# Banded attention: another order of scores, value products and turns on TensorE, and moved work at the begin and end of its stage

## The chip, the cores and the metric

The kernel runs on one core of one Trainium2 chip. The metric is device time in microseconds. Times before: 1762.6 us, the median of three runs (1760.01 to 1762.82).

## The reference

One layer of a hybrid block on 1024 latent tokens of width 1024, with 256 context tokens: a projection to all branches, differential attention, pooling, windowed attention, a merge, and a feed-forward block. The change touches the third branch, windowed attention with sink logits, and what is computed beside it:

```python
rel = jnp.arange(band)[None, :] - WA_BLOCK - jnp.arange(WA_BLOCK)[:, None]
band_ok = jnp.abs(rel) <= WA_WINDOW
def one(args):
    i, qblk = args
    kb = lax.dynamic_slice_in_dim(kp, i * WA_BLOCK, band, axis=1)
    vb = lax.dynamic_slice_in_dim(vp, i * WA_BLOCK, band, axis=1)
    ...
    s_band = jnp.einsum('bqkgd,bjkd->bkgqj', qblk, kb).astype(jnp.float32) * scale
    s_band = jnp.where(ok, s_band, -jnp.inf)
    s_ctx = jnp.einsum('bqkgd,bjkd->bkgqj', qblk, kc).astype(jnp.float32) * scale
    p = sink_softmax(jnp.concatenate([s_band, s_ctx], axis=-1), sink_g)
    vv = jnp.concatenate([vb, vc], axis=1)
    return jnp.einsum('bkgqj,bjkd->bqkgd', p.astype(v.dtype), vv)
```

There are 8 query heads in 2 key heads, a head is 64 wide, a block is 128 queries, and a query sees the blocks at its left and right, its own, and the context.

## The kernel before

The stage is `window`. It cuts the work into 32 units: key head (16 units each), block of 128 queries, pair of heads. A unit has two heads, s = 0 and 1, and four or five tiles of 128 keys: two of context, and two (first and last block) or three of the band. The units run in a software pipeline of 35 steps. On TensorE, step i before the change issues the scores of unit i for both heads (lines 1634 to 1645, five matmuls a head, the last adds the mask), the value products of unit i-2 (line 1673, 2 x 4 or 2 x 5 pairs of matmuls of 64 columns in the array), and the turns of unit i-1 (line 1659): transposes of the two heads' exponentials and of one tile of reciprocals, in three parts of at most four tiles.

The other engines follow their own programs of the same steps. ScalarE does the exponential of head 0, the exponential of head 1 (line 1752), the exponential of the sinks (1757), the copy of part 0 of the turns of unit i-1 out of PSUM (1763), and the high part of the output of unit i-2 (1769). VectorE does the maximum of head 0 (1914), in the first nine units the low part of an output (1859), the reciprocals of unit i-1 (1926) and their widening (1852), the maximum of head 1, in the first nine the sinks (1846), the output of unit i-2 (1942), and the copies of parts 1 and 2 (1931). From unit 9 on POOL does the low part, the widening and the sinks.

Order between engines is by semaphores alone. The four upper PSUM banks form a ring (`ring`, `slot`, `use`): the value product, the three turn parts, and in some steps a fifth user take the next bank each, and each waits until the bank's last user has been copied out. Fifth users are the conditioning sums in steps 0 and 1, the row sums in steps 4, 5, 5 and 6 (line 1696), a pool product in steps 7, 10, ... 28 (helper lines 78 to 80) and a branch turn in steps 9, 12, ... 30 (line 1681). A product waits besides for the copies of all three of its turn parts.

At the stage's begin POOL adds and multiplies two rows (lines 1869 and 1870, twice) and splits the pool weights into a high and a low part (1873, 1875), for which the sync queue (SP) loads them (1592). ScalarE takes a square root (1832) whose reciprocal VectorE forms (1984). At its end the first merge product (`merge_first`, helper lines 106 to 109) is issued in two pieces in steps 32 and 33.

Of the kernel before, what the change touches and what calls it, by code (L numbers as in the profile page):

```python
# [1449 lines left out]
def window(nc, sem, block, banks, io, keep):  # L1450
# [6 lines left out]
    UN = WA_KV * KU  # L1457
# [6 lines left out]
    with ExitStack() as ctx:  # L1464
# [103 lines left out]
        @block.sync  # L1568
        def _(sp):
            def load_v(kv, landed):  # L1570
                v = io["vals"][DA_HEADS].rearrange("t p (g d) -> g p t d", g=WA_KV)[kv]
                sp.dma_start(val[kv][:, 2:TT, :], v[:, 0:TL, :]).then_inc(landed, 16)
                sp.dma_start(val[kv][:, 0:2, :], v[:, TL:TT, :]).then_inc(landed, 16)

            sp.wait_ge(*att["cleared"])
            sp.sem_inc(passed, 1)
            load_v(0, v_in)
            for done in ("products", "last_out", "squares"):
                sp.wait_ge(*att[done])
            for i in range(2):  # L1580
                sp.dma_start(row_in_sb[2 * i], io["b_ada"][0:1, (2 + 3 * i) * D:(3 + 3 * i) * D].to_broadcast([P, D])).then_inc(rows_in, 16)
                sp.dma_start(row_in_sb[2 * i + 1], io["norm_g"][1 + 2 * i:2 + 2 * i, :].to_broadcast([P, D])).then_inc(rows_in, 16)
            sp.wait_ge(*att["late"])
            for n in range(2):
                for part, a in ((0, 0), (1, HD)):
                    src = io["qk"][10 + n, part].rearrange("(s d) n -> d s n", d=HD)
                    for s, y in enumerate((y_hi, y_lo)):
                        sp.dma_start(y[2][a:a + HD, 2 + n, :].bitcast(F32), src[:, s, 0:SEQ]).then_inc(q1_in, 16)
            sp.wait_ge(sums_read, 4)
            load_v(1, v1_in)  # L1590
            load_window_keys(io, sp, 1, (kc1[:, 0, :], kc1[:, 1, :]), CTX, SEQ, kc1_in)
            sp.dma_start(pw[:], io["pool_w"]).then_inc(pw_in, 16)
            sp.wait_ge(late_ready, 1)
            sp.dma_start(io["late_row"], late_row[0:1]).then_inc(late_out, 16)
            for n in range(2):
                for s in range(2):
                    sp.wait_ge(sc_done[s], (10, 16)[n])
                cols = slice(CTX + n * HALF, CTX + (n + 1) * HALF)
                load_window_keys(io, sp, 1, (k_st[:, cols], k_sw[:, cols]), HALF, n * HALF, k1_in[n])
            for j in range(2):  # L1600
                sp.dma_start(keep["b_raw"][j][:], io["w_br"][j]).then_inc(keep["b_in"][j], 16)
            sp.wait_ge(late_out, 16)

        @block.tensor
        def _(pe):
# [2 lines left out]
                pe.wait_ge(free[b], used + 1)  # L1608
                return b, banks[4 + b]

            def scores(u):
                kv, blk, pair = at(u)
                if u == 0:
                    pe.wait_ge(qk_in, 16 * (8 + WA_GROUP))
                    pe.wait_ge(const_ready, 2)
                if u == KU:
                    pe.wait_ge(q1_in, 16 * 8)
                    pe.wait_ge(kc1_in, 16 * 4)
                    pe.wait_ge(k1_in[0], 16 * 4)
                if u == KU + 6:  # L1620
                    pe.wait_ge(k1_in[1], 16 * 4)
                band = tiles_of(u)[2]
                width = (len(tiles_of(u)) - 2) * P
                for s in range(2):
                    if u == 0:
                        for done in att["exps"][s]:
                            pe.wait_ge(*done)
                    else:
                        pe.wait_ge(exp_done[s], u + 1)
                    here = slice(blk * P, (blk + 1) * P)  # L1630
                    q = (y_hi, y_lo)[s][2][:, 2 + pair, here] if kv else q_st[pair][:, s, here]
                    keys = (kc1[:, 0, :], kc1[:, 1, :]) if kv else (k_st[:, 0:CTX], k_sw[:, 0:CTX])

                    pe.matmul(banks[2 * s][:, CTX:HALF], q, keys[0], start=True, stop=False)
                    pe.matmul(banks[2 * s][:, CTX:HALF], q, keys[1], start=False, stop=True)
                    out, cols = banks[2 * s + 1][:, 0:width], slice(band * P, band * P + width)
                    pe.matmul(out, q, k_st[:, cols], start=True, stop=False)
                    pe.matmul(out, q, k_sw[:, cols], start=False, stop=False)
                    sides = slice(0, 3, 2)
                    if width == BAND:  # L1640
                        mm = pe.matmul(out.rearrange("p (a n) -> p a n", n=P)[:, sides, :], ident_r[:],
                                       mask_r[:].rearrange("p (a n) -> p a n", n=P)[:, sides, :], start=False, stop=True)
                    else:
                        m0 = (band - 2 - (blk - 1)) * P
                        mm = pe.matmul(out, ident_r[:], mask_r[:, m0:m0 + width], start=False, stop=True)
                    mm.then_inc(sc_done[s], 1)
# [68 lines left out]
            cond_sums(1)  # L1715
            for i in range(1, STEPS):
                if 2 <= i < UN:
                    scores(i)
                if i == UN + 1:
                    first["product"](pe, 0, range(2, BC))  # L1720
                if 0 <= i - 2 < UN:
                    products(i - 2)
                if i == UN:
                    for s in range(2):
                        pe.wait_ge(exp_done[s], UN + 1)
                    pe.wait_ge(da_lo_ready, GROUPS)
                    first["product"](pe, 0, range(2))
                if 0 <= i - 1 < UN:
                    turn(i - 1)
                if i in POOL_STEPS:  # L1730
# [131 lines left out]
        def _(pool):  # L1862
# [1 line left out]
            pool.memset(ones, 1.0).then_inc(ones_ready, 1)  # L1864
            pool.wait_ge(rows_in, 64)
            ch = Chain(pool, pool_step)
            for i, out in enumerate((gate_row[:], late_row)):
                pool.wait_ge(sums_read, 2 * i + 2)
                ch.link(pool.tensor_tensor(out, out, row_in_sb[2 * i], ALU.add))
                ch.link(pool.tensor_tensor(out, out, row_in_sb[2 * i + 1], ALU.mult))  # L1870
            pool.sem_inc(late_ready, 1)
            pool.wait_ge(pw_in, 16)
            pool.tensor_copy(pw_hi[:], pw[:]).then_inc(pw_ready, 1)
            pool.wait_ge(pw_ready, 1)
            pool.tensor_tensor(pw_lo[:], pw[:], pw_hi[:].bitcast(F32), ALU.subtract).then_inc(pw_ready, 1)
            pool.wait_ge(rms_ready, 1)

            def normed(g):
# [30 lines left out]
        def _(v):  # L1909
# [39 lines left out]
            for i in range(STEPS):  # L1949
# [20 lines left out]
                if i < UN:  # L1970
                    maximum(ch, i, 1)
                    if i < POOL_FROM:
                        sinks(v, i)
                if i == 3:
                    v.wait_ge(*att["squares"])
                    v.tensor_scalar(ss[:], ss[:], 1.0 / DA_V, EPS, ALU.mult, ALU.add).then_inc(ss_ready, 1)
# [2 lines left out]
                if 0 <= i - 1 < UN:  # L1979
                    copy_out(i - 1, 1)  # L1980
                    copy_out(i - 1, 2)
                if i == 3:
                    v.wait_ge(root_ready, 1)
                    v.reciprocal(ss[:], ss[:]).then_inc(rms_ready, 1)


def merge_first(nc, sem, banks, keep):
# [1381 lines left out]
```

## Time and profile before

| | |
|---|---|
| median of the runs | 1762.6 us |
| profiled execution | 1762.77 us, span 1760.8 us |
| mean granted clock of TensorE | 0.994 |
| TensorE busy | 1715.9 us, 97% |
| VectorE busy | 1212.0 us, 69% |
| ScalarE busy | 808.4 us, 46% |
| POOL busy | 809.2 us, 46% |

The first four rows are of the whole kernel; the stage that is changed covers some 170 us of it, near 715 to 887 us from the span's start. TensorE is busy nearly always, in the sense that some matmul is in flight; a gap on it is time in which it waited. The granted clock is a share of full speed. In rows in order of time a matmul's length is its way through the array, longer than the distance to the next matmul's start, so costs are taken from start to start.

### The profile page before, as it was taken

What the parts mean: (1) busy time and instruction counts of PE and PEld (TensorE: products, weight loads), DVE (VectorE), ACT (ScalarE), POOL (GpSimd) and SP (SyncE); (2) the same over time, 40 slices, a digit from 0 to 9 for tenths busy, and PEclk for the clock granted to TensorE, in tenths of its full rate; (3) what the DMA queues carried; (4) which work ended last, traced back from release to release, by engine and by line L of the source; (5) the groups of instructions that cost most, each with busy time, mean ns of one, the idle gap of its engine ahead of it and who ended that gap; (6) DMA issues with size and microseconds to landing.
All of it is one profiled execution on the core that took longest, in us unless ns stands there. A gap on an engine that the chain in (4) does not pass through costs nothing. (4 is left out here: it accounts for less than half of the span.)

```text
span 1760.8 us, 25882 instructions
## 1 busy us (share of the span) xinstructions
PE 1715.9 (97%) x9180; PEld 1448.3 (82%) x9180; DVE 1212.0 (69%) x1651; ACT 808.4 (46%) x1593; POOL 809.2 (46%) x579
## 2 busy tenths in 40 slices
PE   8999999999998999989999999899999999999998
PEld 6997888888887999878888878678888888878886
DVE  3628688879958999778733466875665665575767
ACT  3435333435637888657711155633333333354453
POOL 1407577776533899435522232465555555400000
PEclk9999999999999999989999999999999999999999
DMA  9233233435767655512053332132233233386734
GB/s 352 86 109 137 98 120 154 154 147 182 273 170 212 171 139 139 159 32 73 2 196 120 120 133 89 73 131 96 95 116 134 95 107 119 119 280 214 250 100 179
DMA packets 98568, 249.87 MB, mean 142 GB/s; under 512 B 12321, under 2 KB 26017, under 8 KB 98338
## 3 DMA queue, kind: packets, MB, share of 16 engines
q1 hardware_dynamic: 98466, 248.52, 42.3%
q8 instruction: 63, 1.03, 0.2%
q14 instruction: 39, 0.32, 0.1%
HBM read 183.07 MB, written 65.41 MB: 141 GB/s over the span
## 5 line engine op out<-in xcount | busy, mean ns | idle before, releaser
L750 POOL TENSOR_TENSOR ring<-raw_w,ring 128x512 fp32r<-128x512 f32 x120 | 186.9, 1575 | 137.5 <-ACT ring L621 137.5
L78 PE MATMUL psum<-h_hi,ring 128*128 128x512 f32 x400 | 155.9, 390 | 2.7 <-ACT z L667 2.0
L80 PE MATMUL psum<-h_hi,ring 128*128 128x512 f32 x400 | 155.6, 389 | 0.0
L79 PE MATMUL psum<-h_lo,ring 128*128 128x512 f32 x400 | 155.6, 389 | 0.0
L78 PE MATMUL psum<-u_slot 128*128 128x512 f32 x308 | 120.4, 391 | 1.3 <-DVE u_slot L2976 1.2
L80 PE MATMUL psum<-u_slot 128*128 128x512 f32 x308 | 120.2, 390 | 0.0
L79 PE MATMUL psum<-u_slot 128*128 128x512 f32 x308 | 119.9, 389 | 0.0
L621 ACT ACTIVATE ring<-raw_w 128x512 fp32r<-128x512 f32 x120 | 72.5, 625 | 100.2 <-DVE raw_w L915 31.8
L1406 DVE TENSOR_REDUCE mx<-psum 128x1 f32<-128x1280 f32 x64 | 95.1, 1487 | 7.6 <-PE psum L1292 6.9
L1339 ACT ACTIVATE e<-psum,neg_m 128x1280 f32<-128x1280 f32 x64 | 85.0, 1328 | 31.2 <-DVE neg_m L1407 31.2
L2575 POOL TENSOR_TENSOR cut_lo<-i_raw,cut_hi 128x512 fp32r<-128x512 f32 x44 | 66.8, 1519 | 59.3 <-ACT cut_hi L2430 59.3
L78 PEld LDWEIGHTS psum<-h_hi,ring 128*128 128x128 f32 x400 | 75.1, 188 | 19.2 <-issue 3.9
L2575 POOL TENSOR_TENSOR cut_lo<-stage,cut_hi 128x512 fp32r<-128x512 f32 x40 | 59.8, 1495 | 64.0 <-ACT cut_hi L2430 64.0
L80 PEld LDWEIGHTS psum<-h_hi,ring 128*128 128x128 f32 x400 | 75.1, 188 | 15.7
L79 PEld LDWEIGHTS psum<-h_lo,ring 128*128 128x128 f32 x400 | 75.1, 188 | 15.6
L1291 PE MATMUL psum<-k_st,q_st 128*128 128x512 f32 (+1 forms) x192 | 74.3, 387 | 5.8 <-ACT e L1339 4.8
L1305 PE MATMUL psum<-val,at 128*128 128x128 f32 x640 | 76.7, 275 | 0.0
L78 PE MATMUL psum<-b_hi,cut_hi 128*128 128x512 f32 x176 | 69.5, 395 | 4.8 <-POOL cut_lo L2575 2.3
L1305 PEld LDWEIGHTS psum<-val,at 128*128 128x128 f32 x640 | 74.0, 192 | 0.0
L78 PE MATMUL psum<-m_parts,i_hi 128*128 128x512 f32 x176 | 69.6, 395 | 0.3 <-PE psum L80 0.3
L78 PE MATMUL psum<-i_t_hi,cut_hi 128*128 128x512 f32 x176 | 68.5, 389 | 1.3 <-POOL i_lo L2575 1.3
L78 PEld LDWEIGHTS psum<-u_slot 128*128 128x128 f32 x308 | 57.8, 188 | 14.5 <-DVE u_slot L2981 1.6
(419 smaller groups left out, 5198.7 us busy)
## 6 DMA issues: line engine op xcount, KB each, us to landing
raw_w<-in_w_pairs SPq DMA_DIRECT2D x40, 512.0 KB, 4.7
qk_dram<-room SPq DMA_DIRECT2D x26, 512.0 KB, 3.6
room<-in_w_ada SPq DMA_DIRECT2D x24, 512.0 KB, 5.7
gates_dram<-ost SPq DMA_DIRECT2D x24, 512.0 KB, 3.0
b_g<-gates_dram SPq DMA_DIRECT2D x8, 1536.0 KB, 7.5
stage<-in_w_ff SPq DMA_DIRECT2D x22, 512.0 KB, 5.9
i_raw<-in_w_ff SPq DMA_DIRECT2D x22, 512.0 KB, 5.0
f_dram<-h SPq DMA_DIRECT2D x22, 512.0 KB, 3.4
```

What stands on the lines that cost most here:

```text
L78: pe.matmul(out, sh, mh, start=first, stop=False, skip_group_check=onto)
L79: pe.matmul(out, sh, ml, start=False, stop=False, skip_group_check=onto)
L80: return pe.matmul(out, sl, mh, start=False, stop=last, skip_group_check=onto)
L621: act.activation(w_hi[i], source(p, i), ACT.Copy).then_inc(w_hi_ready, 1)
L750: pool.tensor_tensor(w_lo[i], source(p, i), w_hi[i].bitcast(F32), ALU.subtract).then_inc(w_lo_ready, 1)
L1291: pe.matmul(out, q, k_st[j][:, s, c0:c0 + w], start=True, stop=False)
L1305: mm = pe.matmul(bank[:, 2 * P:3 * P], at[t % 2][:, k, :], val[t // TL % 2][:, k, :], start=(k == 0), stop=(k == TT - 1))
L1339: act.activation(e[i % 2][s][:], psum[:, 3 * s * HALF:3 * s * HALF + TOK], ACT.Exp, scale=SCALE, bias=neg_m[:, i % 2, s:s + 1], accum_out= ...
L1406: ch.link(v.tensor_reduce(mx[:, s:s + 1], psum[:, 3 * s * HALF:3 * s * HALF + TOK], AX.X, ALU.max))
L2575: pool.tensor_tensor(f_lo[i], source(q, i), f_hi[i].bitcast(F32), ALU.subtract).then_inc(fw_lo_ready, 1)
```

## The change

On TensorE the scores of the two heads are taken apart: a step now issues the scores of head 0, the value products, the scores of head 1, and the turns. The names in the rows are the program's: `y_hi` and `y_lo` hold the queries of the second key head, `k_st` and `wa_kc` keys, `we` the exponentials, `wpt` the turned ones. TensorE, a step of a unit with five tiles, before:

```order
L1635 MATMUL psum<-wa_kc,y_hi 128x256
L1637 MATMUL psum<-k_st,y_hi 128x384
L1638 MATMUL psum<-k_st,y_hi 128x384
L1641 MATMUL psum<-wa_mask_r,wa_ident_r 128x2x128
L1634 MATMUL psum<-wa_kc,y_lo 128x256
L1635 MATMUL psum<-wa_kc,y_lo 128x256
L1637 MATMUL psum<-k_st,y_lo 128x384
L1638 MATMUL psum<-k_st,y_lo 128x384
L1641 MATMUL psum<-wa_mask_r,wa_ident_r 128x2x128
L1673 MATMUL psum<-wpt,wa_val 64x128 x10
L1659 MATMUL psum<-ident,we 128x128 x10
L1659 MATMUL psum<-ident,wpt 128x128
```

TensorE, the same place, now:

```order
L1635 MATMUL psum<-wa_kc,y_hi 128x256
L1637 MATMUL psum<-k_st,y_hi 128x384
L1638 MATMUL psum<-k_st,y_hi 128x384
L1641 MATMUL psum<-wa_mask_r,wa_ident_r 128x2x128
L1673 MATMUL psum<-wpt,wa_val 64x128 x10
L1634 MATMUL psum<-wa_kc,y_lo 128x256
L1635 MATMUL psum<-wa_kc,y_lo 128x256
L1637 MATMUL psum<-k_st,y_lo 128x384
L1638 MATMUL psum<-k_st,y_lo 128x384
L1641 MATMUL psum<-wa_mask_r,wa_ident_r 128x2x128
L1659 MATMUL psum<-ident,we 128x128 x10
L1659 MATMUL psum<-ident,wpt 128x128
```

The ten rows of the products stood behind both heads' scores, and stand between them now; the turns stay last.

At the stage's end, in step 32 (`b_hi_first` and `b_lo_first` are merge weights), TensorE before:

```order
L1659 MATMUL psum<-ident,wpt 128x128
L1673 MATMUL psum<-wpt,wa_val 64x128 x8
L106 MATMUL psum<-y_hi,b_hi_first 128x512
L107 MATMUL psum<-y_lo,b_hi_first 128x512
L106 MATMUL psum<-y_hi,b_hi_first 128x512
L107 MATMUL psum<-y_lo,b_hi_first 128x512
L109 MATMUL psum<-y_hi,b_lo_first 128x512 x2
```

and now:

```order
L1645 MATMUL psum<-wa_mask_r,wa_ident_r 128x256
L1659 MATMUL psum<-ident,we 128x128 x8
L1659 MATMUL psum<-ident,wpt 128x128
L106 MATMUL psum<-y_hi,b_hi_first 128x512
L107 MATMUL psum<-y_lo,b_hi_first 128x512
L106 MATMUL psum<-y_hi,b_hi_first 128x512
L107 MATMUL psum<-y_lo,b_hi_first 128x512
```

The product of unit 30 stood ahead of the first piece of the merge product, and stands behind it now.

POOL at the stage's begin (`gate_row` and `early` are the two rows, `wa_pw` the pool weights), before:

```order
L1869 TENSOR_TENSOR gate_row<-gate_row,rows 128x1024
L1870 TENSOR_TENSOR gate_row<-gate_row,rows 128x1024
L1869 TENSOR_TENSOR early<-early,rows 128x1024
L1870 TENSOR_TENSOR early<-early,rows 128x1024
L1873 CAST pool_w_hi<-wa_pw 128x512
L1875 TENSOR_TENSOR pool_w_lo<-wa_pw,pool_w_hi 128x512
L1881 TENSOR_TENSOR on<-o,o_squares 128x512
```

and now:

```order
L1872 TENSOR_TENSOR gate_row<-gate_row,rows 128x1024
L1873 TENSOR_TENSOR gate_row<-gate_row,rows 128x1024
L1877 CAST pool_w_hi<-wa_pw 128x512
L1879 TENSOR_TENSOR pool_w_lo<-wa_pw,pool_w_hi 128x512
L1872 TENSOR_TENSOR early<-early,rows 128x1024
L1873 TENSOR_TENSOR early<-early,rows 128x1024
L1887 TENSOR_TENSOR on<-o,o_squares 128x512
```

The split of the pool weights has moved ahead of the second row. On the sync queue the load of the pool weights has moved ahead of six loads for the second key head, and on VectorE the reciprocal of the squares from the end of step 3 to step 5, ahead of its output. The programs of ScalarE and of the other steps are as they were.

```diff
--- before.py
+++ after.py
@@ -1587,9 +1587,9 @@
                     for s, y in enumerate((y_hi, y_lo)):
                         sp.dma_start(y[2][a:a + HD, 2 + n, :].bitcast(F32), src[:, s, 0:SEQ]).then_inc(q1_in, 16)
             sp.wait_ge(sums_read, 4)
+            sp.dma_start(pw[:], io["pool_w"]).then_inc(pw_in, 16)
             load_v(1, v1_in)
             load_window_keys(io, sp, 1, (kc1[:, 0, :], kc1[:, 1, :]), CTX, SEQ, kc1_in)
-            sp.dma_start(pw[:], io["pool_w"]).then_inc(pw_in, 16)
             sp.wait_ge(late_ready, 1)
             sp.dma_start(io["late_row"], late_row[0:1]).then_inc(late_out, 16)
             for n in range(2):
@@ -1608,7 +1608,7 @@
                 pe.wait_ge(free[b], used + 1)
                 return b, banks[4 + b]
 
-            def scores(u):
+            def scores(u, heads=range(2)):
                 kv, blk, pair = at(u)
                 if u == 0:
                     pe.wait_ge(qk_in, 16 * (8 + WA_GROUP))
@@ -1621,7 +1621,7 @@
                     pe.wait_ge(k1_in[1], 16 * 4)
                 band = tiles_of(u)[2]
                 width = (len(tiles_of(u)) - 2) * P
-                for s in range(2):
+                for s in heads:
                     if u == 0:
                         for done in att["exps"][s]:
                             pe.wait_ge(*done)
@@ -1715,16 +1715,18 @@
             cond_sums(1)
             for i in range(1, STEPS):
                 if 2 <= i < UN:
-                    scores(i)
+                    scores(i, [0])
                 if i == UN + 1:
                     first["product"](pe, 0, range(2, BC))
-                if 0 <= i - 2 < UN:
-                    products(i - 2)
                 if i == UN:
                     for s in range(2):
                         pe.wait_ge(exp_done[s], UN + 1)
                     pe.wait_ge(da_lo_ready, GROUPS)
                     first["product"](pe, 0, range(2))
+                if 0 <= i - 2 < UN:
+                    products(i - 2)
+                if 2 <= i < UN:
+                    scores(i, [1])
                 if 0 <= i - 1 < UN:
                     turn(i - 1)
                 if i in POOL_STEPS:
@@ -1864,15 +1866,19 @@
             pool.memset(ones, 1.0).then_inc(ones_ready, 1)
             pool.wait_ge(rows_in, 64)
             ch = Chain(pool, pool_step)
-            for i, out in enumerate((gate_row[:], late_row)):
+
+            def row(i, out):
                 pool.wait_ge(sums_read, 2 * i + 2)
                 ch.link(pool.tensor_tensor(out, out, row_in_sb[2 * i], ALU.add))
                 ch.link(pool.tensor_tensor(out, out, row_in_sb[2 * i + 1], ALU.mult))
-            pool.sem_inc(late_ready, 1)
+
+            row(0, gate_row[:])
             pool.wait_ge(pw_in, 16)
             pool.tensor_copy(pw_hi[:], pw[:]).then_inc(pw_ready, 1)
             pool.wait_ge(pw_ready, 1)
             pool.tensor_tensor(pw_lo[:], pw[:], pw_hi[:].bitcast(F32), ALU.subtract).then_inc(pw_ready, 1)
+            row(1, late_row)
+            pool.sem_inc(late_ready, 1)
             pool.wait_ge(rms_ready, 1)
 
             def normed(g):
@@ -1971,6 +1977,9 @@
                     maximum(ch, i, 1)
                     if i < POOL_FROM:
                         sinks(v, i)
+                if i == 5:
+                    v.wait_ge(root_ready, 1)
+                    v.reciprocal(ss[:], ss[:]).then_inc(rms_ready, 1)
                 if i == 3:
                     v.wait_ge(*att["squares"])
                     v.tensor_scalar(ss[:], ss[:], 1.0 / DA_V, EPS, ALU.mult, ALU.add).then_inc(ss_ready, 1)
@@ -1979,9 +1988,6 @@
                 if 0 <= i - 1 < UN:
                     copy_out(i - 1, 1)
                     copy_out(i - 1, 2)
-                if i == 3:
-                    v.wait_ge(root_ready, 1)
-                    v.reciprocal(ss[:], ss[:]).then_inc(rms_ready, 1)
 
 
 def merge_first(nc, sem, banks, keep):
```

## Rows read from the trace of the kernel before

**Rows 1.** Stretches: length, busy us (instructions) by engine, granted clock, DMA share, GB/s

```profile
730.32:778.76 48.44, 39.04 (x291) 31.71 (x290) 33.59 (x89) 24.34 (x58) 12.38 (x8) 0.86 0.41 105
778.76:872.78 94.02, 93.79 (x935) 84.86 (x933) 77.20 (x203) 71.84 (x184) 45.20 (x85) 1.00 0.13 41
872.78:886.40 13.62, 12.54 (x107) 10.35 (x106) 6.18 (x16) 5.77 (x15) 6.40 (x10) 1.00 0.01 1
745.00:749.00 4.00, 3.78 (x16) 3.00 (x18) 2.53 (x8) 2.22 (x7) 0.00 (x0) 0.66 0.48 100
```

**Rows 2.** Waits of the window stage: who for whom; us, times, longest

```profile
PE psum L78 <- POOL pool_w_lo L1875: 3.5, 1, 3.5
PE psum L1659 <- DVE wpt L1852: 3.1, 3, 1.2
PE psum L1696 <- DVE wpt L1942: 2.4, 2, 1.2
DVE o_squares L1984 <- ACT o_squares L1832: 1.7, 1, 1.7
```

**Rows 3.** Order of time, TensorE, step 20: start, us, what [idle before <-releaser]

```profile
824.49 0.48 PE L78 MATMUL psum<-y_hi,pool_w_hi 128*128 128x512 f32 x1
...
825.26 0.28 PE L1634 MATMUL psum<-wa_kc,y_hi 128*128 128x256 f32 x1
...
825.84 0.28 PE L1641 MATMUL psum<-wa_mask_r,wa_ident_r 128*128 128x256 f32 x1
...
826.75 1.31 PE L1673 MATMUL psum<-wpt,wa_val 128*64 128x128 f32 x20
828.00 1.31 PE L1659 MATMUL psum<-ident,we 128*128 128x128 f32 x10
...
829.17 0.37 PE L1634 MATMUL psum<-wa_kc,y_hi 128*128 128x256 f32 x1
```

**Rows 4.** The same step on VectorE and ScalarE

```profile
826.16 0.82 DVE L1914 TENSOR_REDUCE wmx<-psum 128x1 f32<-128x640 f32 x1 [0.56 <-PE psum L1641]
...
828.38 0.28 DVE L1942 TENSOR_TENSOR wpt<-psum,wpt 128x128 f32<-128x128 f32 x1
...
827.27 0.80 ACT L1752 ACTIVATE we<-psum,wneg_m 128x640 f32<-128x640 f32 x1 [0.41 <-DVE wneg_m L1916]
...
828.50 0.80 ACT L1752 ACTIVATE we<-psum,wneg_m 128x640 f32<-128x640 f32 x1 [0.35 <-DVE wneg_m L1916]
...
829.38 0.59 ACT L1763 ACTIVATE wpt<-psum 128x512 f32<-128x512 f32 x1
```

**Rows 5.** The same view near the stage's end: POOL, VectorE, TensorE

```profile
875.99 1.27 POOL L1887 TENSOR_TENSOR y_lo<-on,y_hi 128x512 fp32r<-128x512 f32 x1
...
876.50 0.89 DVE L1931 COPY wpt<-psum 128x512 f32<-128x512 f32 x2 [0.61 <-PE psum L1659]
...
877.64 1.09 PE L1673 MATMUL psum<-wpt,wa_val 128*64 128x128 f32 x16 [1.07 <-DVE wpt L1931]
```

**Rows 6.** ScalarE, the exponential of a unit with four key tiles

```profile
811.89 0.69 ACT L1752 ACTIVATE we<-psum,wneg_m 128x512 f32<-128x512 f32 x1
```

**Rows 7.** The opening: TensorE, VectorE, sync queue, POOL

```profile
751.68 1.88 PE L1696 MATMUL psum<-late_rows,early 128*128 128x512 f32 x4
...
756.33 2.08 DVE L1852 COPY wpt<-wrec 128x128 f32<-128x128 f32 x1
...
762.68 0.38 SPq L1572 DMA_DIRECT2D wa_val<-vals_dram  x1
...
766.57 0.59 SPq L1592 DMA_DIRECT2D wa_pw<-in_pool_w  x1
...
769.52 0.61 POOL L1873 CAST pool_w_hi<-wa_pw 128x512 fp32r<-128x512 f32 x1 [1.90 <-DMA wa_pw<-in_pool_w]
770.21 1.26 POOL L1875 TENSOR_TENSOR pool_w_lo<-wa_pw,pool_w_hi 128x512 fp32r<-128x512 f32 x1
```

**Rows 8.** TensorE's 20 products at the lower clock

```profile
748.71 1.78 PE L1673 MATMUL psum<-wpt,wval 128*64 128x128 f32 x20
```

## The prediction

> **What bounds the kernel now.** I read the table of stages first. The window stage splits into an opening (steps 2 to 8, 48.44 us), a steady part (steps 9 to 30, 94.02 us) and an end (13.62 us) [rows 1]. A step i issues the scores of unit i, the value products of unit i-2 and the turns (transposes) of unit i-1, so a steady step lasts 94.02/22 = 4.27 us. In the steady part TensorE is busy 93.79 of 94.02 us at clock 1.00: there it is the bound. In the opening it is busy 39.04 of 48.44 us, at a mean granted clock of 0.86, so it waits for others and then also runs at the lower of its two levels (1.2 and 2.4 GHz).
>
> Next come the waits [rows 2]: 3.5 us at the first pool product for the split of the pool weights, 3.1 us at the last turn of a unit for the widened reciprocals, 2.4 us at row sums for the output that frees their bank. VectorE lost 1.7 us waiting for the square root. That is the opening. After step 9 almost nothing stands there.
>
> Last I read one steady step on TensorE [rows 3] and on VectorE and ScalarE [rows 4] in order of time, because the new order changes who waits there. The reader is to see in [rows 4] the exponential of head 1 at 828.50, and right behind it on ScalarE, in program order, the copy of turn part 0 at 829.38. The products of the same unit need that copy. Today it ends at 829.97, while TensorE is busy with the scores of both heads of the next step from 829.17, 10 matmuls lasting from 825.26 to 826.75 in the step shown, 1.49 us, plus 0.08 after turns. So the products are due at about 830.75: the copy is hidden with about 0.8 us to spare.
>
> **Part one: the order in the steady steps.** Nothing is added or removed, no matmul is longer. But the scores of head 1 now stand behind the products, so (a) the products have only one head's scores, 0.66 to 0.78 us, in front of them instead of two, and (b) the exponential of head 1 comes later than before relative to the turns. ScalarE's order is not changed: it still does exponential head 0, exponential head 1, sinks, and only then the copy of part 0. That closes a loop: scores of head 1 (step i), maximum, exponential, copy of part 0 (unit i-1), products (unit i-1, step i+1), scores of head 1 (step i+1). Its links for a unit with five key tiles:
> - last matmul of a head's scores to the reduce: 825.84 to 826.16, 0.32 [rows 3, 4]
> - reduce to its exponential: 826.16 to 827.27, 1.11 [rows 4]
> - exponential of head 1 to the copy of part 0: 828.50 to 829.38, 0.88 [rows 4]
> - that copy: 0.59 [rows 4]
> - end of a copy to the products it releases: the row 876.50 + 0.89 = 877.39 to 877.64, 0.25 [rows 5]
> - the 20 products: 826.75 to 828.00, 1.25 [rows 3]
> - scores of one head up to their last matmul: 825.26 to 825.84, 0.58 [rows 3]
>
> The sum is 4.98 us. The other way round TensorE has, between the last matmul of the scores of head 1 and the next products, only 0.11 + turns 1.17 + 0.78 = 2.1 us of work, and the copy is there after 3.15: about 1 us of idle per step. VectorE's own copies of parts 1 and 2 don't set it: its output starts 0.12 ahead of the exponential of head 1 (828.38 against 828.50), so at 0.32 + 1.11 - 0.12 = 1.31, ends at 1.59, and both copies, 1.16 for five tiles (0.89 for four, [rows 5]), end at 2.75. With four key tiles the exponential takes 0.69 for 0.80 [rows 4, 6], 0.11 less; the reduce (512 keys for 640) is about 0.13 shorter, the products (16 for 20) 0.22, the scores 0.11: the loop is 4.41.
>
> A pool product (0.77: 824.49 to 825.26 [rows 3]) uses the bank that the output on VectorE frees, at 1.59 + 0.15 = 1.74 after that last matmul. Then 1.74 + 0.77 + 0.78 + 0.1 = 3.4 against the copy's 3.15: 0.25 more in each of 7 steps, 1.75. A branch turn, four transposes, is shorter and fits.
>
> Of the 22 steps I count 17 at five tiles and 5 at four: 17 x 4.98 + 5 x 4.41 + 1.75 = 108.5, against 94.0. **Term A is +14.5 us.** Its bounds: 0 if the loop is somehow hidden, 14.5 plus about 22 if the clock stays low (second rival). I take the loop, since every link has a row in this very stage.
>
> **Part two: the new places at the begin.** Seven steps of the loop, with the first not held back (about 0.9 less), are 34.0 us. What comes on top, step by step:
> - Steps 4 and 5, +2.7. Two row sums took 1.32 us, from 751.68 to the scores at 753.00 [rows 7], so three are 2.0, behind the bank's release at about 1.74; the rest is my allowance for ScalarE's function tables, which it loads around the square root. The reciprocal that VectorE waited 1.7 us for now stands in step 5, where its input is long there; what is late next is the row sum's bank.
> - Step 6, +2.9: the widening copy on VectorE took 2.08 us, until the add on POOL had ended (756.33 + 2.08 = 758.41) [rows 7], and the maximum of head 1 and all that hangs on it stood behind. That add stays where it is. With the fourth row sum and some half clock I take 2.9.
> - Step 7, +2.2: pool weights. The issue moves ahead of six DMAs of the sync queue. It was issued at 766.57 and used at 769.52, 2.95 later; the first of the six went out at 762.68, and there it stands now, 3.9 us sooner [rows 7], and on POOL the split (769.52 to 770.21, and 1.26) stands ahead of the two adds of the second row. TensorE waits about 2.2 instead of 3.5. The six loads behind it are wanted from step 16 on: no cost.
> - Step 8, +0.25. The second row's adds now overlap this step and the reciprocals' users; the late row goes out some 5 us later, and is wanted in step 9 by ScalarE's branch copy, which is about as late as that: nothing, or up to 1 us.
>
> Sum 34.0 + 8.05 = 42.05 against 48.44: **term B is -6.4 us**, bounds -12 (neither row sums nor half clock cost anything) to -1 (the clock is as low as before).
>
> **Part three: the end.** Before, the products of unit 30 waited 1.07 us for VectorE's copy [rows 5]. Now the first half of the merge product (2.87 us) stands before them; but it needs the low part of the last branch, on POOL behind the sinks of the last unit. These end about 0.32 + 1.11 + 0.2 = 1.6 us after the last score; the subtract takes 1.27 [rows 5]. So it starts about 2.9 us after the scores, of which the turns cover 1.1: the wait of 1.07 becomes one of about 1.8. From the start of the last scores I get 0.1 + 0.5 + 0.2 + 1.25 + 0.5 + 2.9 + 2.87 + 1.03 + 0.96 + 2.87 + 1.1 = 14.3 to 14.7 against 13.62. **Term C is +1.0**, bounds -1.1 to +2.
>
> **Sum.** +14.5 - 6.4 + 1.0 = +9.1 us. What follows is bound by TensorE without a gap, so the shift is carried to the end. The profiled execution took 1762.77 us (span 1760.8), 0.2 over the median 1762.6; I forecast 1772, own range 1766 to 1778.
>
> **Rivals.**
> 1. Faster than before: the loop never decides. ScalarE has 0.41 and 0.35 us of idle ahead of its exponentials [rows 4], and DVE's second reduce used to queue behind the first; if spreading them let the copy of part 0 start before TensorE comes to the products (no later than 1.3 us after the last score; the links say 2.3), term A is 0 to +1 and the time is 1757. Against: the links are a chain, none can start earlier. Chance 0.08.
> 2. The clock falls in the steady part. After 745 TensorE ran four us at 0.66 [rows 1], behind turns and two waits of up to 1.2 us of [rows 2]. At the lower level 20 products took 1.78 for 1.31 [rows 8] and a head's scores about twice 0.58. The loop would be about 1.0 longer: 22 us if always, 11 if half the time, 1783 to 1794. For: now every step has turns and then a wait. Against: scores stand between turns and wait here, the gap is a single one of about 1 us, and the like gap at 877 left the clock at 1.00. Chance 0.14.
> 3. The loop is only half as dear (some 0.45 us a step, because a released product starts sooner than 0.25 or the reduce sooner than 0.32): A is +7, the time 1764. Chance 0.13.
>
> Rival 2 is what the Trainium skill would have (TensorE: Matmul & The Clock Gate, "A second HAM failure mode: psum-queue depth-cycling"): a TensorE that idles briefly between groups of matmuls in every iteration is seen to swing between both clock levels. By that rule it would be about 1788; the trace has full clock through the small gaps of the steady part and half clock only after the pairs of long ones, so I keep it a rival.
>
> **How the numbers follow.** Forecast 0.65, rivals 0.08, 0.14 and 0.13. The range 1763 to 1786 leaves out rival 1, the slow half of rival 2 and little of rival 3. A measurement of this kernel tells about 0.2%, 3.5 us: slower has the forecast, rival 2 and a part of rival 3, 0.82; the same 0.10; faster 0.08.
>
> **What would show it.** In the steady part of the new profile TensorE idles about 1 us per step before line 1673, released by ScalarE's copy (line 1765 now), and a step lasts about 5.0 us. The wait at the first pool product is near 2 us, VectorE's wait for the square root is gone, the opening is 42 us. I am wrong if TensorE has no such wait, or if the granted clock in the steady part is under 0.95.

## The result and the profile of the changed kernel

The changed kernel takes 1776.48 us (median of 4 runs, 1774.01 to 1779.46), the kernel before in the same series 1762.53. The ratio is 1.0079, with a 95% interval of 1.0065 to 1.0093: slower by 0.8%. Forecast were 1772.0, with a range of 1763 to 1786. The profiled execution took 1775.1 us (span 1773.1, mean granted clock 0.995), 12.3 more than that of before.

First the stretches, cut at the same points as [rows 1]: opening, steady part and end (length, then busy us of TensorE, its weight loads, VectorE, ScalarE, POOL, granted clock, DMA share, GB/s).

```profile
732.40:775.24 42.84, 34.84 (x292) 28.70 (x290) 32.34 (x85) 22.83 (x54) 12.35 (x7) 0.96 0.45 119
775.24:884.70 109.46, 98.78 (x934) 86.29 (x932) 80.26 (x208) 72.37 (x186) 44.75 (x85) 1.00 0.10 35
884.70:899.33 14.63, 12.78 (x108) 10.35 (x106) 5.46 (x16) 6.19 (x17) 6.71 (x10) 1.00 0.00 1
```

The opening went from 48.44 to 42.84 us (-5.6), the steady part from 94.02 to 109.46 (+15.4), the end from 13.62 to 14.63 (+1.0). Together +10.8. In the steady part the same matmuls are issued, the clock is 1.00 as before, and TensorE now leaves 10.7 us unused where it left 0.2. The other 5.0 us are busy time (98.78 for 93.79) of the same instructions. About 2.2 of them are the first score of head 1, which now follows another group and takes 0.22 to the next matmul instead of 0.12, 22 times. For the rest I have only an estimate: the last matmul ahead of a gap counts for its whole way through the array, 0.28 in the rows below, and not for the 0.12 to the next one's start, which over some 21 gaps makes about 3.

The waits of TensorE name the owners (total us, times, longest). This is the steady part alone:

```profile
PE psum L1673 <- ACT wpt L1765: 5.5, 7, 1.0
PE psum L1681 <- DVE wpt L1948: 2.4, 7, 0.8
PE psum L1673 <- DVE wpt L1937: 1.4, 1, 1.4
PE psum L78 <- DVE wpt L1948: 1.2, 7, 0.2
```

In the kernel before TensorE idled 0.2 us in all of this stretch. Over the opening and the end the list has these too:

```profile
PE psum L78 <- POOL pool_w_lo L1879: 2.2, 1, 2.2
PE psum L106 <- POOL y_lo L1893: 1.9, 1, 1.9
PE psum L1659 <- DVE wpt L1854: 1.0, 1, 1.0
```

The wait for the pool weights was 3.5 and is 2.2, the last turns' wait for the reciprocals was 3.1 and is 1.0, and VectorE's wait for the square root (1.7 in [rows 2]) is gone.

How the steady part fills 15 us with only seven waits at the products is to be seen in order of time. These are the rows of TensorE and of its partners for one step without a branch turn or a pool product (start, us, what [idle before <-releaser]):

```profile
832.79 0.28 PE L1641 MATMUL psum<-wa_mask_r,wa_ident_r 128*128 128x256 f32 x1
...
834.21 0.80 ACT L1754 ACTIVATE we<-psum,wneg_m 128x640 f32<-128x640 f32 x1 [1.26 <-DVE wneg_m L1922]
...
835.09 0.58 ACT L1765 ACTIVATE wpt<-psum 128x512 f32<-128x512 f32 x1
...
835.73 1.31 PE L1673 MATMUL psum<-wpt,wa_val 128*64 128x128 f32 x20 [0.76 <-ACT wpt L1765]
...
837.66 0.28 PE L1641 MATMUL psum<-wa_mask_r,wa_ident_r 128*128 128x256 f32 x1
...
837.98 0.82 DVE L1920 TENSOR_REDUCE wmx<-psum 128x1 f32<-128x640 f32 x1 [1.02 <-PE psum L1641]
...
839.09 0.80 ACT L1754 ACTIVATE we<-psum,wneg_m 128x640 f32<-128x640 f32 x1 [1.75 <-DVE wneg_m L1922]
...
839.97 0.59 ACT L1765 ACTIVATE wpt<-psum 128x512 f32<-128x512 f32 x1
```

This is the chain of the prediction, link for link. From the last matmul of head 1's scores to the reduce 0.32 (837.66 to 837.98), to the exponential 1.11, to the copy of part 0 0.88 (839.09 to 839.97, and 834.21 to 835.09). The copy ends at 835.67 and the products start at 835.73, then 1.24 for them and 0.69 for a head's scores. Against [rows 3, 4] the next rows of TensorE show what it costs; they are the products of four successive steps:

```profile
840.70 1.31 PE L1673 MATMUL psum<-wpt,wa_val 128*64 128x128 f32 x20
...
850.75 1.31 PE L1673 MATMUL psum<-wpt,wa_val 128*64 128x128 f32 x20 [0.76 <-ACT wpt L1765]
```

Those between start at 835.73 (above) and 845.88. So a step without extra work takes 4.88 us (830.85 to 835.73), the one with a branch turn 4.97 (835.73 to 840.70), the one with a pool product 5.18 (840.70 to 845.88), and the next plain one 4.87 again. In the kernel before the same three were 4.00 (826.75 to 830.75), 4.44 (to 835.19) and 4.69 (to 839.88). Before, a step was as long as its work; now all steps are about as long as the loop. Only one in three shows a long wait at the products. In the other two TensorE has already waited at the turn or at the pool product, for VectorE's output of the same chain:

```profile
839.40 0.63 PE L1681 MATMUL psum<-ident,on 128*128 128x128 f32 x4 [0.25 <-DVE wpt L1948]
...
844.28 0.50 PE L78 MATMUL psum<-y_hi,pool_w_hi 128*128 128x512 f32 x1 [0.16 <-DVE wpt L1948]
```

Last the end. The products of unit 30 do not wait any more; the first half of the merge product waits instead, for POOL's subtract behind the last unit's sinks:

```profile
888.90 1.27 POOL L1893 TENSOR_TENSOR y_lo<-on,y_hi 128x512 fp32r<-128x512 f32 x1
...
890.45 0.47 PE L106 MATMUL psum<-y_hi,b_hi_first 128*128 128x512 f32 x1 [1.85 <-POOL y_lo L1893]
```

### The profile page after: what moved, and what is told of

It reads as the page before. It is cut to its first block and busy times, and to the rows that moved or that the text cites. A ratio compares the mean times of both kernels' runs of the same rounds, so it can differ in the third digit from the quotient of the medians.

```text
span 1773.1 us, 25885 instructions
## 1 busy us (share of the span) xinstructions
PE 1718.1 (97%) x9180; PEld 1448.8 (82%) x9180; DVE 1212.0 (68%) x1651; ACT 807.8 (46%) x1593; POOL 809.1 (46%) x579
## 5 line engine op out<-in xcount | busy, mean ns | idle before, releaser
L1920 DVE TENSOR_REDUCE wmx<-psum 128x1 f32<-128x640 f32 (+1 forms) x64 | 50.5, 789 | 42.2 <-PE psum L1641 28.9
L1754 ACT ACTIVATE we<-psum,wneg_m 128x640 f32<-128x640 f32 (+1 forms) x64 | 49.1, 768 | 58.0 <-DVE wneg_m L1922 56.4
```

The costliest lines, as they stand in the source:

```text
L1754: act.activation(e[u % 2][s][:, 0:keys], psum[:, 2 * s * HALF + CTX:2 * s * HALF + CTX + keys], ACT.Exp, scale=SCALE, bias=neg_m[:, u % 2, ...
L1920: ch.link(v.tensor_reduce(mx[:, s:s + 1], psum[:, 2 * s * HALF + CTX:2 * s * HALF + CTX + keys], AX.X, ALU.max))
```

## The experiments

Times are medians; each ratio is against the kernel before on the same chip, with its 95% interval. Lengths of the stage are from the first matmul of the scores of unit 2, unit 9 and unit 31 and the first matmul of the merge product behind the last products, as above. They come from one profiled execution each.

**1. The order alone.** The kernel before with TensorE's new order and nothing else.

```
-  scores(i)
+  scores(i, [0])
   ...
   products(i - 2)
   ...
+  scores(i, [1])
   turn(i - 1)
```

> Only the new order on TensorE (scores of head 0, products, scores of head 1, turns), with the old places at the stage's begin and end. Theory (the loop over ScalarE's copy of part 0 sets the step): steady part (steps 9 to 30) about 109 us against 94.0, opening about 48 as before (its waits are others'), end +0.8; in all +15.5 us, about 1778. Rival (the order costs little, and most of the 14 us comes from the moved places or from work ahead of the stage): under +5 us.

Measured: 1780.05 us (1779.26 to 1782.52), ratio 1.0096 (1.008 to 1.0111). Opening 47.69, steady part 108.88, end 14.08. In its steady part the waits of TensorE are:

```profile
PE psum L1673 <- ACT wpt L1765: 5.4, 7, 0.9
PE psum L1681 <- DVE wpt L1944: 2.4, 7, 0.8
PE psum L1673 <- DVE wpt L1933: 1.0, 1, 1.0
```

The list has the pool products too, with 1.2 in 7 waits as in the changed kernel. The order alone makes the whole loss, +14.9 of steady part, with the same owners. The opening stays near that of before (48.44), so it is the new places that shorten it.

**2. The places alone.** The changed kernel with the scores of both heads together again.

```
-  scores(i, [0])
+  scores(i)
   ...
-  scores(i, [1])
```

> Only the new places at the begin and the end, with both heads' scores ahead of the products in every step as before. Theory: steady part 94 to 95 us, opening about 40 against 48.4 (pool weights, reciprocal of the squares, and with these less half clock), end as before; in all -7 us, about 1755, and both parts add up to the change (+15.5 - 7 against a measured +14 would leave some 5 us to explain). Rival (the places bring nothing, since the next wait is as late): within 2 us of before.

Measured: 1758.75 us (1755.52 to 1761.67), ratio 0.9973 (0.9963 to 0.9983): faster than before. Opening 40.86, steady part 95.30, end 13.63. The loop is gone from the waits. The gain is 5.0 us where about 7 had been expected. The opening is 0.9 longer than expected, and the steady part is 1.3 longer than before, since its first step takes 5.82 instead of 4.53. Just ahead of that step TensorE waits for VectorE's widening of reciprocals, and within it for ScalarE:

```profile
774.88 0.33 PE L1659 MATMUL psum<-ident,wpt 128*128 128x128 f32 x1 [1.19 <-DVE wpt L1852]
776.78 0.39 PE L1634 MATMUL psum<-k_st,k_sw 128*128 128x256 f32 x1 [0.86 <-ACT we L1752]
```

Why VectorE is late there, experiment 6 shows.

**3. ScalarE's copy first.** The changed kernel, but ScalarE copies part 0 of the turned weights between its two exponentials. If the place behind the second exponential makes the loop, the wait must move.

```
   exp(i, 0)
+  if 2 <= i and i - 1 < UN: copy_out(i - 1, 0)
   exp(i, 1)
   ...
   sinks(i)
-  copy_out(i - 1, 0)
+  if i == 1: copy_out(0, 0)
```

> The changed kernel, with ScalarE's copy of turn part 0 ahead of its exponential of head 1. Theory: the copy is out of the loop, but VectorE's copies of parts 1 and 2 end only 0.15 us a step earlier, behind the maximum of head 1, so the step falls from 4.98 to about 4.83 us and the kernel by about 3.5 us (1773). Rival (ScalarE's copy is the only thing in the way): the idle of about 1 us a step goes, 12 to 15 us less, 1762. The wait before the products should now be put down to VectorE's copy.

Measured: 1777.63 us (1773.45 to 1777.98), ratio 1.0068 (1.0054 to 1.0082). That is the time of the changed kernel; the expected gain of some 3.5 us did not come. Steady part 110.18. The wait did move:

```profile
PE psum L1673 <- DVE wpt L1940: 6.7, 8, 1.7
PE psum L1681 <- DVE wpt L1951: 2.2, 6, 0.8
PE psum L78 <- DVE wpt L1951: 1.2, 7, 0.2
```

One step in order of time shows that the chain through VectorE is as long as the one through ScalarE:

```profile
835.89 0.28 PE L1641 MATMUL psum<-wa_mask_r,wa_ident_r 128*128 128x256 f32 x1
...
836.21 0.82 DVE L1923 TENSOR_REDUCE wmx<-psum 128x1 f32<-128x640 f32 x1 [0.80 <-PE psum L1641]
...
837.40 1.15 DVE L1940 COPY wpt<-psum 128x512 f32<-128x512 f32 x2
...
838.80 1.31 PE L1673 MATMUL psum<-wpt,wa_val 128*64 128x128 f32 x20 [0.72 <-DVE wpt L1940]
```

From the last matmul of the scores to the products it takes 2.91 us (835.89 to 838.80), 0.25 of which lies between the end of the copy (838.55) and the first product. Through ScalarE it was 2.94 in the changed kernel (832.79 to 835.73), with only 0.06 behind the copy. Both ends of the fork come at nearly the same time, so taking one away bares the other: 4.84 us a plain step for 4.88. The steps with a pool product keep 5.15 to 5.17, as they wait for VectorE's output in both kernels.

The length of the whole steady part hides that small gain. Its first step took 7.99 us here, for 6.45 in the changed kernel, and its products ran slowly:

```profile
779.89 1.91 PE L1673 MATMUL psum<-wpt,wval 128*64 128x128 f32 x20 [1.71 <-DVE wpt L1940]
```

The granted clock was 0.57 from 780 to 784, behind a wait of 1.71 us; in experiment 7 the wait at the same place was 1.71 as well, and the four us behind it ran at 1.00. Without the first step the steady part is 102.19 us here and 103.01 in the changed kernel: the edit is worth 0.8 us, a quarter of the 3.5 expected. The single cause "ScalarE's order" was thus too narrow: it is the distance from head 1's scores to the next products, by either engine.

**4. Turns ahead of head 1.** The changed kernel with the turns put ahead of head 1's scores. This leaves less work between those scores and the next products. If the loop holds, the turns' time must come on top.

```
   products(i - 2)
-  scores(i, [1])
   turn(i - 1)
+  scores(i, [1])
```

> The changed kernel, with the turns of unit i-1 also ahead of the scores of head 1 (scores head 0, products, turns, scores head 1). Theory: the loop takes in the turns, 1.2 us: 4.98 + 1.2 = 6.1 to 6.2 us a step at five tiles, steady part about 135 us against 109.5, opening some 5 us more, in all +30 us, about 1806, if the clock holds. Rival (what counts is only how much TensorE work stands before the products, which is unchanged here): no change against the changed kernel, within 3 us.

Measured: 1820.42 us (1817.75 to 1822.39), ratio 1.0324 (1.0308 to 1.034). Opening 53.46, steady part 141.14, end 17.10. The direction was expected and the size was only in part: +44 over the changed kernel for an expected +30. Its waits and its stretches:

```profile
PE psum L1673 <- ACT wpt L1765: 13.6, 7, 2.1
PE psum L1681 <- DVE wpt L1948: 11.7, 8, 1.8
PE psum L78 <- DVE wpt L1948: 9.4, 7, 1.4
```

```profile
730.10:783.56 53.46, 39.40 (x291) 31.66 (x290) 30.69 (x84) 23.09 (x54) 13.69 (x11) 0.87 0.37 95
783.56:924.70 141.14, 104.18 (x933) 90.87 (x932) 80.75 (x208) 72.47 (x186) 44.81 (x85) 0.95 0.08 27
```

Here the granted clock does fall in the steady part, to a mean of 0.95, with a gap of 1.2 to 2.2 us in every step. One set of products took 2.35 us instead of 1.31:

```profile
805.16 2.35 PE L1673 MATMUL psum<-wpt,wval 128*64 128x128 f32 x20 [1.96 <-ACT wpt L1765]
```

Three steps took 18.5 us where no slow stretch fell into them (from 858.30 on, by the starts of the scores: 8.03 + 6.45 + 3.99), and 20.1 where one did (9.64 + 6.44 + 4.01). The changed kernel has 15.0. So the loop grew by 3.5 us per three steps, nearly the turns' time of 1.2 in each, as forecast for a clock that holds. That gives 25 us over 22 steps, and the measured steady part is 31.7 longer: most of the extra is loop, and the rest is clock. Four of the seven long waits for ScalarE's copy had a slow stretch behind them. The length of the wait does not tell which, as it was the same 1.96 us at the slow products above and at these, at full clock:

```profile
861.13 1.31 PE L1673 MATMUL psum<-wpt,wa_val 128*64 128x128 f32 x20 [1.96 <-ACT wpt L1765]
```

**5. The begin alone.** The kernel before with the new places of its begin (pool weights, the second row's adds, the reciprocal) and the old end. The edit is that part of the diff of the change and no more; the order of TensorE is the old one, its end included.

> Only the new places at the begin (pool weights, reciprocal); TensorE's order as before in all steps and at the end. Theory: the end's new place is worth nothing, for its wait of 1.07 us only changes its owner, so this runs within 1 us of the kernel with all new places (-5 us against before, opening 41 us). Rival (the end's place is what brought the 5 us): within 1.5 us of before.

Measured: 1758.36 us (1755.3 to 1759.5), ratio 0.996 (0.9947 to 0.9974). Opening 41.16, steady part 95.29, end 13.62. Beside experiment 2 (1758.75, end 13.63) the end's new place is worth nothing with the old order: a wait of 1.1 us at the products of unit 30 comes back and one of 0.9 at the merge product goes.

**6. The rows in quarters.** Experiment 2, with POOL's adds and products on 128x1024 cut into four of 128x256. In [rows 7] a copy on VectorE ended at 758.41, and POOL's multiply of the first row at 758.33 (the prediction called it the add). If VectorE is held for as long as POOL's instruction lasts, shorter instructions must free it.

```
-  ch.link(pool.tensor_tensor(out, out, row_in_sb[2 * i], ALU.add))
-  ch.link(pool.tensor_tensor(out, out, row_in_sb[2 * i + 1], ALU.mult))
+  for j, op in enumerate((ALU.add, ALU.mult)):
+      for q in range(4):
+          c = slice(q * D // 4, (q + 1) * D // 4)
+          (ch.link if q == 3 else ch.did)(pool.tensor_tensor(out[:, c], out[:, c], row_in_sb[2 * i + j][:, c], op))
```

> The kernel with only the new places, with POOL's four adds and multiplies of rows (128x1024, 2.4 us each) cut in quarters of 256. Theory (a VectorE copy or subtract in SBUF that meets a running POOL instruction ends only with it, so what counts is the length of that instruction): the widening of 2.07 us at 757.75 and the subtract of 2.13 at 771.54 fall to under 1 us, TensorE's waits of 1.03 and 1.19 us behind them go, 2 to 3 us less than the kernel with only the new places, 1756. Rival (they share bandwidth in proportion, whatever the instruction's length): the same time as that kernel.

Measured: 1755.85 us (1754.95 to 1759.34), ratio 0.9955 (0.9942 to 0.9969). Opening 39.72, steady part 94.80, end 13.64. First experiment 2, VectorE's and POOL's rows:

```profile
757.75 2.07 DVE L1852 COPY wpt<-wrec 128x128 f32<-128x128 f32 x1
...
764.81 0.23 DVE L1852 COPY wpt<-wrec 128x128 f32<-128x128 f32 x1
...
771.54 2.13 DVE L1859 TENSOR_TENSOR y_lo<-wpt,y_hi 128x128 fp32r<-128x128 f32 x1
```

```profile
757.38 2.36 POOL L1871 TENSOR_TENSOR gate_row<-gate_row,rows 128x1024 f32<-128x1024 f32 x1
...
771.16 2.37 POOL L1871 TENSOR_TENSOR early<-early,rows 128x1024 f32<-128x1024 f32 x1
```

The copy ends at 759.82 and POOL's product at 759.74, the subtract at 773.67 and POOL's at 773.53. The same copy clear of POOL takes 0.23. Now experiment 6:

```profile
756.10 0.65 DVE L1852 COPY wpt<-wrec 128x128 f32<-128x128 f32 x1
...
769.16 0.63 DVE L1859 TENSOR_TENSOR y_lo<-wpt,y_hi 128x128 fp32r<-128x128 f32 x1
```

```profile
752.97 5.74 POOL L1873 TENSOR_TENSOR gate_row<-gate_row,rows 128x256 f32<-128x256 f32 x8 [21.05 <-ACT gate_row L1777]
```

POOL needs 5.74 us for the eight pieces against 4.8 for two whole ones, but VectorE is held 0.65 at most, and both waits of TensorE for the widening copy are gone. The stage gets 1.6 us shorter than in experiment 2, 1.1 of it in the opening and 0.5 in the steady part. This is the lowest ratio of all: 0.45% under the kernel before, and about 1.2% under the changed one (0.9955 against 1.0079). Against experiments 2 and 5 its interval overlaps theirs, so there the rows above show the gain and the times alone do not.

**7. The changed kernel again.** Nothing edited: 1.5 us of the profile's 12.3 lie in the stretch between unit 0 and unit 2, whose code is the same. A rival said that the new order lengthens it.

> The changed kernel once more, with nothing altered, to see what of its +14 us is the stage (10.85 us in the profile, from the scores of unit 2 to the merge's next matmul) and what varies from one execution to the next ahead of it (2.08 us in the profile). Theory: the stage is 166.9 us again within 0.5, the stretch ahead (start of unit 0 to unit 2) anywhere from 17 to 20 us, and the median 11 to 14 us over before. Rival (the change lengthens the stretch ahead as well, by 2 us): that stretch is 18.9 us again and the median +14.

Measured: 1776.50 us (1774.74 to 1779.26), ratio 1.0066 (1.0053 to 1.008). Opening 43.54, steady part 109.71, end 16.20. The stretch took 17.76 this time, against 18.86, and over all profiles it goes from 16.81 (experiment 4, with the new order) to 19.98 (experiment 3), with the old order from 16.83 to 19.63: it does not follow the order. What was missed is the stage: 169.45 us, where 166.9 within 0.5 had been expected. Most of the difference is the end, 16.20 for 14.63: behind a like wait the clock fell.

```profile
891.00:895.00 4.00, 3.60 (x11) 2.88 (x12) 0.29 (x2) 0.64 (x2) 3.30 (x5) 0.68 0.00 0
```

```profile
891.39 0.47 PE L106 MATMUL psum<-y_hi,b_hi_first 128*128 128x512 f32 x1 [1.86 <-POOL y_lo L1893]
...
893.63 0.63 PE L107 MATMUL psum<-y_lo,b_hi_first 128*128 128x512 f32 x1
```

A matmul of 512 columns that took 0.39 right behind the wait takes 0.63 two us later. After a wait of 1.85 in the first profile, nothing of that sort happened.

**8. The reciprocal alone.** The kernel before with VectorE's reciprocal moved from step 3 to step 5, as in the change.

```
+  if i == 5:
+      v.wait_ge(root_ready, 1)
+      v.reciprocal(ss[:], ss[:]).then_inc(rms_ready, 1)
   ...
-  if i == 3:
-      v.wait_ge(root_ready, 1)
-      v.reciprocal(ss[:], ss[:]).then_inc(rms_ready, 1)
```

> The kernel before, with only VectorE's reciprocal of the squares moved from step 3 to step 5. Theory: the wait of 1.7 us for the square root goes, and with it TensorE's waits at 743 and 745 and the half clock behind them; opening 44.5 to 45.5 for 48.4, -3 us, 1760. Rival (the pool weights bring all of the opening's gain, since the row sums wait anyway): within 1 us of before.

Measured: 1760.08 us (1757.85 to 1762.95), ratio 0.9983 (0.9974 to 0.9993). The opening is 45.94, 2.5 shorter. The stretch that ran at 0.66 in [rows 1] runs at full clock, and the pool weights are now the long wait:

```profile
745.00:749.00 4.00, 3.75 (x37) 2.98 (x37) 3.73 (x12) 2.75 (x9) 0.00 (x0) 1.00 0.30 60
```

```profile
PE psum L78 <- POOL pool_w_lo L1875: 4.4, 1, 4.4
```

Of the opening's gain of 7.3 us with the old order (48.44 to 41.16 in experiment 5), the reciprocal makes a third and the earlier weights the larger part of the rest: their wait goes from 4.4 to 1.3 there, and to 2.4 in experiment 2, whose opening has the same code. The third edit, the second row's adds behind the split of the weights, was not run by itself.

## Why the prediction was right, step by step

**Term A, the steady part: +14.5 forecast, +15.4 measured. Shown.** Experiment 1 has the loss with the order alone, experiment 2 has none of it without the order. Five links of the seven came out within 0.01 us. Two did not: the products started 0.06 behind ScalarE's copy and not 0.25, which I had read at a VectorE copy [rows 5], and the scores of one head took 0.69 behind the products instead of 0.58, as their first matmul takes 0.22 to the next one and not 0.12. The plain loop was forecast at 4.98 and is 4.88. The steps with a pool product were forecast at 5.23 and are 5.16 to 5.19 between five-tile steps. With scores of four key tiles, 4.60 and 4.62 behind 20 products and 4.35 behind 16 were measured; the sum had 4.41 for all. That the term lies within 0.9 is partly luck, as five-tile loops came out 0.1 too dear and four-tile ones 0.2 too cheap in the sum, against each other. What made the term larger than its forecast despite the shorter loop are two places that it had not: one step of four tiles waited 0.80 at its branch turn and took 5.03, and the first step took 6.45 us between scores, for 5.77 of later steps with a branch turn. VectorE came late to it, out of a subtract that ended at 773.68 with POOL's product of the second row (773.54):

```profile
771.89 1.79 DVE L1861 TENSOR_TENSOR y_lo<-wpt,y_hi 128x128 fp32r<-128x128 f32 x1
```

```profile
777.64 0.62 PE L1673 MATMUL psum<-wpt,wval 128*64 128x128 f32 x7 [1.45 <-DVE wpt L1937]
```

POOL's row is not the whole of this. In experiment 1 the same subtract met no POOL instruction and took 0.28, and TensorE still waited 1.02 there, in a step of 6.02. So the row costs about 0.4 us of the first step, and the rest comes with the order.

"About 1 us of idle per step before line 1673, released by ScalarE's copy" was right for one step in three only, with 0.76. In the other two the idle time, or the extra work, stands at the branch turn and the pool product ahead. I had said that a branch turn "is shorter and fits"; it waits for VectorE's output 0.25 us and makes the step 0.09 longer. The length of a step was right where the place of the wait was not.

**What the term blamed.** The prediction put the loop on ScalarE's program order, and said that VectorE's copies, which end at 2.75, don't set it. The 3.15 that they seem to be far from holds 0.25 from ScalarE's copy to the products: the copies' ends were forecast 0.15 apart (2.75 and 2.90). In the changed kernel they are 0.23 apart (835.44 and 835.67), but the products start 0.06 behind ScalarE's copy and 0.25 behind VectorE's, so that as TensorE sees them the two chains differ by 0.03 (2.94 and 2.91 us, experiment 3). For the size of the change that made no difference. For a repair it decides: moving ScalarE's copy brings 0.8 us of 15.

**Term B, the opening: -6.4 forecast, -5.6 measured (42.84 for 42.05).** By step, the scores of units 2 to 9 lie 4.06, 4.97, 6.53, 6.66, 7.5, 7.6 and 5.52 us apart. The loop had 4.1 and 4.98 for the first two. Steps 4 and 5 were to take 12.7 together and took 13.2, step 6 7.9 and 7.5, step 7 7.2 and 7.6, step 8 5.2 and 5.5. The wait for the weights was forecast at about 2.2 and was 2.20. Step 8 is where the cost of overlapping POOL's second row was put at nearly nothing; [rows 7] had already a 2.08 us copy in the first row's overlap, and the second overlap did the same, in the subtract of 1.79 that precedes the 1.45 us wait. I had carried that price to step 6 and not to step 8. In the kernel before, the second row held a copy for 2.07 us too (at 765.63), but there TensorE waited for the pool weights anyway. It is the one place where the row was in view and not used, worth about 0.7 us: 0.3 in step 8 and the 0.4 of the first steady step.

**Term C, the end: +1.0 forecast, +1.0 measured.** The wait of 1.07 became one of 1.85 (about 1.8 forecast), with the owner named. With the old order the new place costs and gives nothing (experiments 2 and 5), and with the new order and the old place (experiment 1) the end is 14.08, with a wait of 1.4: about half of the price is the order's and half the place's on top of it. It can also cost 2.6 if the clock falls behind the wait, as in experiment 7.

**The sum** was +9.1; the stage shows +10.8. Ahead of unit 2 the profile has 2.1 more, 0.6 up to unit 0 and 1.5 in a stretch that varies by 3 us from execution to execution; behind the stage it has 0.6 less, which makes its 12.3. Terms A and B both came out about 0.9 dearer than forecast, and their errors add up. The medians are 14 apart in the first series, and the ratio of the second (1.0066) is about 12. Experiments 1 and 5 sum to +16.3 - 5.5 = +10.8. What makes medians a few us longer than the stage's difference is not settled. A fallen clock behind a wait, as in experiment 7, would do it in part; it was not looked for over many profiles.

**The rivals.** That the loop never decides is refuted by 5.5 us of waits at the products and a step of 4.88 for 4.00. That it is half as dear is refuted by the same numbers: 0.88 more for a plain step. That the clock falls in the steady part did not happen in this kernel: 1.00 over 109 us, in both profiles of it and in experiment 1, with a gap of 0.7 to 1.0 in every third step, smaller ones between, and one of 1.0 to 1.7 in the first. Two experiments show that it can happen in this stage: number 3 once, behind a gap of 1.71, and number 4 four times, with a gap of 1.2 to 2.2 in every step. The price of rival 2 was too low: the 1.78 us of [rows 8] lie only partly in the slow stretch (0.61 from 748.71 to 750.00, 1.00 behind that), and those of the slow stretch from 805.16 on took 2.35 in experiment 4. What the Trainium skill reports of one kernel (TensorE: Matmul & The Clock Gate, "A second HAM failure mode: psum-queue depth-cycling") is thus seen in experiment 4 and not in the change: small gaps in every iteration were no sufficient cause.

## What to carry to other kernels

Splitting a group of matmuls so that consumers can start sooner pays only if what comes behind it does not close a loop: write down the chain from the piece moved later to the next matmul that needs its result, and compare it with the work that TensorE has in between, before counting any gain. If the chain has two ends on two engines, measure both as TensorE sees them; removing one bares the other. And look for a VectorE instruction on SBUF that ends together with a long POOL instruction: cutting POOL's instruction into pieces costs POOL some time (0.9 us on 4.8 here) and gives VectorE back most of its wait.

## What was not expected of the hardware

- A 128x128 copy or subtract on VectorE between SBUF operands, 0.23 to 0.28 us by itself, took 2.07 and 2.13 us beside a POOL add or product on 128x1024 and ended within 0.15 us of it. Beside pieces of 128x256 it took 0.65 at most.
- The same wait of 1.85 us at the end left the clock at 1.00 in one execution and was followed by a mean of 0.68 over four us in another. Of the seven long waits at the products in experiment 4, all of 1.8 to 2.1 us, four had a slow stretch behind them and three had none, in one execution. Neither one gap's length nor one execution tells what a gap costs.
- TensorE started 0.06 us behind the end of the ScalarE copy that released it, and 0.25 behind that of the VectorE copy, in the same place of the program. It is not VectorE as such: behind VectorE's output the pool product started after 0.06 and the branch turn after 0.15. Why they differ no run shows.
